# A routed mixture of experts: rows scattered earlier, weights requested later, the overflow list built among the experts

## The reference, cut to what matters

```
grp = argmax(x @ wg + bg);  top_v, top_i = top_k(e_in, 2)
expert = grp * 8 + top_i;   combine = p_grp * softmax(top_v)
rows are sorted by expert and padded to blocks of 128 rows
hb = silu(xb @ w_gate[e]) * (xb @ w_up[e]);   y = hb @ w_down[e]
out[t] = h[t] + sum over its two experts of combine * y
```

## Time and profile before

| | |
|---|---|
| three runs | 3042.2, 3044.1, 3045.62 us; median 3044.1 us |
| profiled execution | 3048.14 us, its span 3046.3 us |
| PE busy over the span | 2782.6 us (91%) |
| VectorE, ScalarE, GpSimd busy | 1670.6, 1199.9, 201.3 us |
| mean TensorE clock granted | 0.961 of full |
| last stage | from 2475 us to the end of the span |

### The profile page before, as it was taken

One profiled execution on the slowest core, in us unless ns is written; L12 is line 12 of the kernel. 1 busy time (PEld: TensorE's weight loads), 2 busy tenths in 40 slices (PEclk: granted clock), 3 DMA queues, 4 the chain that ended last, 5 costly groups with the idle time before them and its releaser, 6 DMA issues. The chain is left out here.

```text
span 3046.3 us, 34519 instructions
## 1 busy us (share of the span) xinstructions
PE 2782.6 (91%) x13088; PEld 2206.3 (72%) x13088; DVE 1670.6 (55%) x2460; ACT 1199.9 (39%) x1670; POOL 201.3 (7%) x183
## 2 busy tenths in 40 slices
PE   7999999999999999979999988999989889489994
PEld 5878778877878787757777787777767668357772
DVE  5687777877742323433243323666666653446664
ACT  4233333333240213634424414545555531245661
POOL 0010111101100000000000000000000000521213
PEclk9999999999999999989999999999999999689997
DMA  5322222222234212021122020000000130979996
GB/s 175 130 94 95 101 70 100 101 101 76 87 135 183 76 51 74 35 61 44 49 69 62 28 77 26 23 15 23 15 23 15 56 79 35 329 272 347 356 374 260
DMA packets 168692, 329.12 MB, mean 108 GB/s; under 512 B 17831, under 2 KB 125480, under 8 KB 154840
## 3 DMA queue, kind: packets, MB, share of 16 engines
q1 hardware_dynamic: 152952, 289.25, 27.4%
q0 software_dynamic: 14720, 34.64, 3.0%
q10 hardware_dynamic: 864, 3.15, 0.3%
HBM read 293.94 MB, written 100.16 MB: 129 GB/s over the span
## 5 line engine op out<-in xcount | busy, mean ns | idle before, releaser
L380 PE MATMUL PS<-UHI,WHI 128*128 128x512 f32 x1008 | 416.6, 413 | 19.7 <-DVE arena L767 15.6
L380 PE MATMUL PS<-ULO,WHI 128*128 128x512 f32 x1008 | 403.5, 400 | 0.0
L380 PE MATMUL PS<-UHI,WLO 128*128 128x512 f32 x1008 | 403.1, 400 | 0.0
L127 DVE TENSOR_TENSOR WLO<-arena,WHI 128x1024 fp32r<-128x1024 f32 x96 | 117.4, 1223 | 241.5 <-ACT WHI L123 241.2
L380 PEld LDWEIGHTS PS<-UHI,WHI 128*128 128x128 f32 x1008 | 192.5, 191 | 71.9 <-issue 24.4
L380 PEld LDWEIGHTS PS<-ULO,WHI 128*128 128x128 f32 x1008 | 192.5, 191 | 46.8 <-issue 4.1
L380 PEld LDWEIGHTS PS<-UHI,WLO 128*128 128x128 f32 x1008 | 192.3, 191 | 47.0
L1388 PE MATMUL PS<-U2HI,WHI 128*128 128x512 f32 x512 | 207.0, 404 | 13.2 <-DVE WLO L127 13.2
L1388 PE MATMUL PS<-U2LO,WHI 128*128 128x512 f32 x512 | 203.1, 397 | 0.0
L1388 PE MATMUL PS<-U2HI,WLO 128*128 128x512 f32 x512 | 203.0, 396 | 0.0
L781 DVE SCALAR_TENSOR_TENSOR RC<-arena,cols,RC 128x1024 f32<-128x1024 f32 x120 | 157.4, 1312 | 9.9 <-issue 0.4
(11 more groups left out here) (444 smaller groups left out, 5839.0 us busy)
## 6 DMA issues: line engine op xcount, KB each, us to landing
arena<-in_w_in SPq DMA_DIRECT2D x88, 512.0 KB, 3.9
xd_dram<-in_x SPq DMA_DIRECT2D x32, 768.0 KB, 6.2
y_dram<-in_x SPq DMA_DIRECT2D x32, 768.0 KB, 6.1
arena<-in_w_gate SPq DMA_DIRECT2D x13, 1024.0 KB, 7.5
arena<-in_w_up SPq DMA_DIRECT2D x13, 1024.0 KB, 11.0
arena<-in_w_down SPq DMA_DIRECT2D x13, 1024.0 KB
arena<-in_w_out SPq DMA_DIRECT2D x32, 256.0 KB, 2.7
RB<-in_w_gate SPq DMA_DIRECT2D x7, 1024.0 KB
```

Of the source, the lines that this page charges most:

```text
L127: return eng.tensor_tensor(dst, src, hi.bitcast(F32), ALU.subtract)
L380: last = pe.matmul(o[:, h * HALF:(h + 1) * HALF], x[:, k, :], y[:, k, h * HALF:(h + 1) * HALF], start=(k == r == 0), stop=(k == ND - 1 and ...
```

## The change

The first batch of scatters (tiles 0 to 3) now stands ahead of the wait for the projection and of the three memsets, which follow it. The load of the weights of block b, for b = 2, 3, 4, waits for the gather of block b-2 instead of for the scatters. The writing of the overflow list is spread over the first eight steps of GpSimd's loop, two DMAs in each, ahead of that step's gather; the list is read back in step 10 and waited for in step 29, where the first overflow block is gathered.

```
-                        sp.wait_ge(s_scat, 16 * 2 * NT)
+                        sp.wait_ge(s_xland[b - 2], 16)
...
-                pool.wait_ge(s_h2p, NT)
-                for k in range(3):
-                    last = pool.memset(XB[k], 0.0)
-                last.then_inc(s_xzero, 1)
                 for n, (m0, m1) in enumerate(BATCHES):
+                    if n == 1:
+                        pool.wait_ge(s_h2p, NT)
+                        for k in range(3):
+                            last = pool.memset(XB[k], 0.0)
+                        last.then_inc(s_xzero, 1)
                     pool.wait_ge(s_rows8, n + 1)
...
-                for u in range(2):
-                    for m in range(NT):
+                def list_tokens(m):
+                    for u in range(2):
                         pool.indirect_dma_start(list_dram, bass.IndirectOffsetOnAxis(ap=LISTROW[:, u, m:m + 1], axis=0),
                                                 PARKI[:, u, m:m + 1], None).then_inc(s_listst, 16)
-                pool.wait_ge(s_listst, 16 * 2 * NT)
-                pool.dma_start(LISTI[:], list_dram[0:NOVER * P].rearrange("(b p) o -> p (b o)", p=P)).then_inc(s_listed, 16)
-                pool.wait_ge(s_listed, 16)
...
                 for b in range(NS):
+                    if b < NT:
+                        list_tokens(b)
+                    elif b == NT + 2:
+                        pool.wait_ge(s_listst, 16 * 2 * NT)
+                        pool.dma_start(LISTI[:], list_dram[0:NOVER * P].rearrange("(b p) o -> p (b o)", p=P)
+                                       ).then_inc(s_listed, 16)
                     if 3 <= b + 3 < NE:
                         rows_in(b + 3)
                     elif b + 3 == NE:
+                        pool.wait_ge(s_listed, 16)
                         pool.wait_ge(s_xgt, NE - 2)
                         gather(XB[NE % 3], LISTI[:, 0:1], s_xover)
```

## The result

Six runs of the changed kernel have a median of 3060.3 us (3058.1 to 3069.9), six of the kernel before 3045.8 us (3042.2 to 3050.1). The ratio is 1.0052, 95% interval 1.0038 to 1.0066: about 15 us slower, where 27.6 us faster was forecast. The profiled execution has a span of 3061.1 us, against 3046.3.

The account below looks back on a forecast made before the run. It took TensorE's work plus the holes between it as the bound. 6.1 + 4.3 + 14.75 + 2.4 = 27.6 us off the profiled 3048.1 gave 3020.5, with the median 4.0 lower at 3016.5; range 3010 to 3025.

Parts of the forecast that it names:

- Part 1: Routing on GpSimd: the first eight scatters are issued earlier, so the scatters land 6.1 us earlier.
- part 2: Start of the experts: weights of blocks 2 to 4 queue behind the first gathers, so gather 0 lands 4.3 us sooner.
- part 3: Before turn 3: gather 3 no longer waits for the whole list and its reading back; TensorE's 14.75 us wait goes.
- part 4: Turn 3 to turn 4 on TensorE: without idleness ahead, the step keeps the full clock, saving 2.4 us.
- the memsets delay nobody: GpSimd's routing: the three memsets, now after the first eight scatters, end before the next row numbers, with 2.7 us of cover.
- the second hole: TensorE's wait of 14.76 us after two experts, said to be made by GpSimd's order alone.
- part 5: Steps 0 to 7: two more list DMAs cost GpSimd 2.6 us before each gather; covered, so nothing in the sum.
- the rival of late weights: First experts: the list's small writes slow weight loads, TensorE waits 6 us, time 3022.5; chance 0.14 in either form.
- The strongest form of the rival: Engines cannot exceed the steady stage's rate, so delayed weight loads stay late; about 12 us gain, 3032; within the 0.14.
- Gathers late behind the list: Steps 2 to 7: gathers over 14.6 us from issue cost six steps each; chance 0.04 partly late, 0.03 slower.

Follow-up runs that it names:

- parked skipped: The changed kernel with a bound on the row number, so tokens that are no overflow are not written to the list; 3016.4 us, ratio 0.9909.
- part 1 alone: The kernel before with only the first eight scatters moved ahead of the memsets; 3039.9 us, ratio 0.9979.
- its own experiment: The kernel that skips the parked tokens, with the weights of blocks 2 to 4 again waiting for the scatters; 3022.1 us, ratio 0.9935.
- the kernels without the close writes: The changed kernel without the list DMAs (0.9906), with parked tokens not written (0.9909), or with the list's integers 64 bytes apart (0.9914).
- the last experiment: The kernel before with only the writing of parked tokens skipped, its sixteen list DMAs in their old place; 3033.8 us, ratio 0.9971.
- the scatters of their own: The kernel that skips parked tokens, plus scatters into unread DRAM tensors in steady steps; a 4-byte pair took the engines from 362 to 77 GB/s.
- the 64-byte list: The changed kernel with the list's integers 64 bytes apart in DRAM instead of 4, same steps and order; 3017.7 us, ratio 0.9914.
- the run of sixteen: The changed kernel with all sixteen list DMAs in one run in step 1, old order, not waited for until step 10; 3021.6 us, ratio 0.9917.

## Why the prediction was wrong

Step by step, in the kernel before, as forecast, and in the two profiles:

| | before | forecast | changed | parked skipped |
|---|---|---|---|---|
| last scatter's issue to first gather's issue | 15.4 | 9.3 | 9.4 | 9.7 |
| first gather's issue to turn 0 | 8.6 | 4.3 | 4.5 | 4.1 |
| turn 0 to turn 3 | 39.8 | 25.0 | 24.3 | 25.0 |
| turn 3 to turn 4 | 12.6 | 10.15 | 15.7 | 10.1 |
| turn 3 to turn 11 | 83.6 | 81.2 | 124.6 | 81.1 |

**Right, part by part.** Part 1 (6.1 us forecast; 6.0 found, 5.1 with part 1 alone), part 2 (4.3; 4.1, and 5.5 in its own experiment) and part 3 (14.75; 14.8 with the parked writes skipped). The low clock behind the hole, part 4, is gone too in that kernel. The sum of 27.6 us is what the kernels without the close writes gained: ratios of 0.9906 to 0.9914 are 26 to 29 us. That the memsets delay nobody held as well. One premise of part 3 was wrong, though its size was right: the second hole was not made by GpSimd's order alone. In the last experiment that order is kept and only the parked writes are gone: the gather of block 3 comes 11 us sooner, and some 11 of the hole's 14.8 us go with them.

**Wrong: the price of the list DMAs in the steady stage, in part 5 and in the rival of late weights.** Part 5 counted what two more DMAs cost GpSimd (2.6 us of issue) and the gather behind them, and put nothing for what they cost the weights. The rival had the right mechanism, small writes that hold up the large ones, and mis-sized it. Its price came from the list of the kernel before, 208 GB/s over 20 us for sixteen DMAs, with the argument that two in 10 us must cost less than one in 1.3 us. The runs show the reverse. A pair in the changed order costs 2.3 MB of transfers, 5.4 us at full rate. The steady stage needs 3.61 MB in 10.15 us, 8.6 us at 420 GB/s, and so has 1.5 us of the step to spare. An estimate from these rows: 8 us at 77 GB/s bring 0.6 MB, the other 3.0 MB take 7.1 us at 420, so a step with a pair takes 15.1 us and loses 5.0; eight lose 40. The steps took 43.4 us more. The strongest form of the rival left 12 us of gain; it was 15 us of loss.

**What I had not read in the diff.** The change also exchanges the loops over the two choices and the tiles. I took the order as free. It decides: with the old order in the same steps the kernel is 19 us faster than before instead of 15 slower. The row was a price for writes 8 bytes apart, and the new code writes 4 bytes apart.

**The other rivals.** Gathers late behind the list did not set the time: ScalarE's waits for weights come first in the changed kernel. That the engines can't carry more than the steady stage shows was the stronger form's ground. The Trainium skill (DMA: Bandwidth & Descriptors, Where 436 GB/s comes from) puts the bound of such transfers near 358 GB/s, though the same section also calls a measured 425 GB/s near the fabric's rate. The runs don't agree with the first figure: behind a stall the engines moved 403 to 422 GB/s, most of it weights.

**Open.** That closeness in DRAM is the cause is shown, by the scatters of their own and by the 64-byte list. Which part of the path serialises such writes, and why reads of weights from elsewhere in DRAM stop with them, is not. The Trainium skill (DMA: Bandwidth & Descriptors, Why small descriptors are slow) puts a fixed few cycles on each small packet; that can't be what is seen here, since the same count of the same size costs nothing 64 bytes apart. Nor do I know how the cost adds up over sixteen in one run: 8-byte pairs lose 0.9 MB each, which would make 7.2 MB or 17 us, and the run of sixteen lost some 5 us of time, part of it hidden by the lead.

## What to carry to other kernels

Before spreading small DMAs among large ones, price them on the DMA engines and not only on the queue that issues them; a stage whose transfers take 8.6 of 10.15 us has no room for a stall in every step. Don't write what nobody reads: by itself the bound that skips the parked tokens gained 8.8 us where the rearrangement lost about 15, and the two together gained some 28. When loops over scatters are exchanged, look at where consecutive writes land, and keep single words that are written in a scatter apart. 64 bytes were enough in the whole kernel; 16 bytes were enough for one DMA, and no pair was measured at that distance.

## What the runs showed of the hardware

- 256 single integers scattered into 1 KB of DRAM, 4 bytes apart, by two DMAs in a row: the core's 16 DMA engines fell from 362 to 77 GB/s for 8 us, with a busy share of 0.95, so the share doesn't tell a stall from work.
- 128 integers 8 bytes apart: 348 to 255 GB/s over 8 us. 16, 32 and 64 bytes apart: 19 GB/s less, 6 more and 1 more than one step earlier. Pairs with rows of 64 and 512 bytes: 16 and 12 less. Stretches of this phase without a scatter range from 332 to 370.
- The share was 1.12 at 56 GB/s in the changed kernel, and one up matrix of 1 MB took 46.3 us from its request to its landing, where the kernel without the parked writes has some 11 to 12.
- Rate behind a stall: 403 to 422 GB/s. In the stretch with 422, 2.85 of the 3.38 MB were weights, HBM to SBUF.
- Sixteen list DMAs and the reading back held the next gather 41.4 us behind the one before it; with the parked writes skipped, the same sixteen DMAs held it 30.4 us.
